# Hybrid Hyena and pooling encoder layer on one core: at the seam to the last stage, two tables asked for later, w_out piece 0 split behind the last unit, two groups reloaded as 120 and 8 partitions

## The reference

```
u    = x * (1 + scale) + shift                     # scale, shift, gate from c
proj = u @ w_in + b_in                             # 1024 -> 3072
v, x1, x2 = short_conv(proj[:, :1536])             # 3 x 512 channels
z = v
for o, g in enumerate((x1, x2)):                   # two long convolutions, 4096-point spectra
    z = g * (irfft(rfft(z) * k_freq[o])[:L] + z * bias[o])
y_h = z * silu(proj[:, 1536:2048])
y_p = pooling_mixer(proj[:, 2048:2560]) * silu(proj[:, 2560:3072])
out = gate * (concat(y_h, y_p) @ w_out + b_out)
h   = layer_norm(alpha * x + out) * ln_g + ln_b
```

## Time and profile before

| | |
|---|---|
| median of 3 runs | 1181.8 us (1180.28, 1181.8, 1186.05) |
| the profiled execution | 1175.66 us, of which the span of the trace 1173.8 us |
| TensorE busy | 1088.2 us, 93% of the span |
| VectorE busy | 850.9 us, 72% |
| ScalarE busy | 584.4 us, 50% |
| SyncE's DMA queue | 266.74 MB, 71.4% of the 16 engines' span |
| last unit's store to bseq asked for | 950.57 us |

### The profile page before, as it was taken

One profiled execution on the slowest core, in us unless ns is written; L12 is line 12 of the kernel. 1 busy time (PEld: TensorE's weight loads), 2 busy tenths in 40 slices (PEclk: granted clock), 3 DMA queues, 4 the chain that ended last, 5 costly groups with the idle time before them and its releaser, 6 DMA issues. The chain is left out here.

```text
span 1173.8 us, 14214 instructions
## 1 busy us (share of the span) xinstructions
PE 1088.2 (93%) x4928; PEld 840.9 (72%) x4928; DVE 850.9 (72%) x1081; ACT 584.4 (50%) x769; POOL 12.5 (1%) x32
## 2 busy tenths in 40 slices
PE   3799789999999999998999999898999779999996
PEld 1278668888888877766888877666788557888885
DVE  6699985555455545649999746554999957989887
ACT  4068864434545444537777635444888753222210
POOL 0001000000000000000000000000000000000000
PEclk8789999999999999999999999999999879999998
DMA  9999855677675435688999568778899999476531
GB/s 341 346 311 288 281 180 167 204 246 236 235 251 171 173 108 196 213 263 225 299 282 285 172 210 263 263 232 252 248 286 297 276 313 324 130 218 185 180 108 54
DMA packets 155132, 273.24 MB, mean 233 GB/s; under 512 B 11503, under 2 KB 49519, under 8 KB 153396
## 3 DMA queue, kind: packets, MB, share of 16 engines
q1 hardware_dynamic: 151605, 266.74, 71.4%
q0 software_dynamic: 3168, 5.51, 2.1%
q10 hardware_dynamic: 288, 0.08, 0.0%
HBM read 178.95 MB, written 98.57 MB: 236 GB/s over the span
## 5 line engine op out<-in xcount | busy, mean ns | idle before, releaser
L177 PE MATMUL u_pp<-uh_uhi,prj_whi 128*128 128x512 f32 x768 | 309.7, 403 | 14.2 <-DVE u_ulo L741 8.7
L179 PE MATMUL u_pp<-uh_uhi,prj_wlo 128*128 128x512 f32 x768 | 305.1, 397 | 0.0
L178 PE MATMUL u_pp<-u_ulo,prj_whi 128*128 128x512 f32 x768 | 304.7, 397 | 0.0
L177 PEld LDWEIGHTS u_pp<-uh_uhi,prj_whi 128*128 128x128 f32 x768 | 145.8, 190 | 57.0 <-issue 14.8
L179 PEld LDWEIGHTS u_pp<-uh_uhi,prj_wlo 128*128 128x128 f32 x768 | 145.7, 190 | 34.4
L178 PEld LDWEIGHTS u_pp<-u_ulo,prj_whi 128*128 128x128 f32 x768 | 146.1, 190 | 32.2
L1282 DVE TENSOR_TENSOR p_alo<-xin_pair,p_ahi 128x1024 fp32r<-128x1024 f32 x32 | 39.2, 1226 | 97.3 <-ACT p_ahi L1219 97.3
L1219 ACT ACTIVATE p_ahi<-xin_pair 128x1024 fp32r<-128x1024 f32 x32 | 33.9, 1060 | 124.0 <-PE p_ps L179 117.0
L593 ACT ACTIVATE fs_khi<-fs_k 128x1024 fp32r<-128x1024 f32 x32 | 34.0, 1062 | 42.2 <-DVE fs_k L570 42.2
L554 PE MATMUL fs_s<-fs_khi,flt_tab 64*128 64x512 f32 x256 | 50.6, 417 | 2.5 <-ACT prj_row L598 2.5
L177 PE MATMUL p_first<-uh_uhi,prj_whi 128*128 128x512 f32 x128 | 51.1, 399 | 1.6 <-DVE prj_wlo L2270 1.6
(11 more groups left out here) (212 smaller groups left out, 2112.0 us busy)
## 6 DMA issues: line engine op xcount, KB each, us to landing
xin_pair<-kseq SPq DMA_DIRECT2D x32, 512.0 KB, 4.3
kfreq<-xin_pair SPq DMA_DIRECT2D x32, 512.0 KB, 5.1
xseq<-p_xo SPq DMA_DIRECT2D x32, 512.0 KB, 7.7
p_k_re<-kfreq SPq DMA_DIRECT2D x64, 256.0 KB, 5.7
p_k_im<-kfreq SPq DMA_DIRECT2D x64, 256.0 KB, 4.9
bseq<-p_out SPq DMA_DIRECT2D x32, 512.0 KB, 5.1
prj_ws<-in_t_win SPq DMA_DIRECT2D x24, 512.0 KB
kseq<-prj_row SPq DMA_DIRECT2D x22, 512.0 KB, 4.1
```

Source lines behind the costliest of these rows:

```text
L177: nc.tensor.matmul(out, w[0], m[0], start=start, stop=False, skip_group_check=True)
L178: nc.tensor.matmul(out, w[0], m[1], start=False, stop=False, skip_group_check=True)
L179: return nc.tensor.matmul(out, w[1], m[0], start=False, stop=stop, skip_group_check=True)
```

## The change

Three edits in the same place.

The two tables of groups 0 and 1 were asked for at step NU - 3; they are asked for at step NU - 1, behind the store of unit 14. Piece 0 of w_out was split by ScalarE at step NU - 2 and by VectorE inside step NU - 1; both are done after the last unit's y has been split. Groups 0 and 1 were loaded whole once the store of the last unit had landed; partitions 0 to 119 are loaded once the store of unit 14 has landed, on both sides of the last store's issue, and partitions 120 to 127 after it. `high(0)` and `high(1)` wait for both parts.

```diff
--- before.py
+++ after.py
@@ -1533,8 +1533,17 @@
                 if tail and step == NU:
                     tail.load_w(sp, 4)
                     tail.load_w(sp, 5)
+                if tail and step == NU:
+                    sp.wait_ge(alo_done, NU)
+                    sp.wait_ge(stored, 16 * (NU - 1))
+                    tail.load_x_stored(sp, 0)
                 if 0 <= step - 1 < NU:
                     store(step - 1)
+                if tail and step == NU - 1:
+                    for n in range(2):
+                        tail.load_tab(sp, n)
+                if tail and step == NU:
+                    tail.load_x_stored(sp, 1)
                 q = plan.due(plan.chunk, step)
                 if q is not None and q % 4 == 2:
                     pj.load_w(sp, q // 4 + 2)
@@ -1547,8 +1556,6 @@
                 if tail and step == NU - 3:
                     tail.chunks_done(sp)
                     tail.load_quad(sp, tail.pq[0], tail.yp, tail.pq_in[0], 0)
-                    for n in range(2):
-                        tail.load_tab(sp, n)
             if tail:
                 gt.finish(sp, 4)
                 end_sync(sp)
@@ -1660,8 +1667,8 @@
                 if tail and step == NU - 2:
                     tail.chunks_done(act)
                     tail.pooled_high(act, 0, tail.pq[0])
+                if tail and step == NU - 1:
                     tail.w_high(act, 0)
-                if tail and step == NU - 1:
                     tail.w_high(act, 1)
                     tail.w_high(act, 2)
                     tail.w_high(act, 3)
@@ -1722,8 +1729,6 @@
                 if 0 <= step < NU:
                     turned(step)
                     add(step)
-                if tail and step == NU - 1:
-                    tail.w_low(dve, 0)
                 q = plan.due(plan.post, step)
                 if q is not None:
                     if q == 4 * gt.first:
@@ -1736,7 +1741,7 @@
                 if 0 <= step < NU:
                     ylow(step)
             if tail:
-                for i in range(1, 4):
+                for i in range(4):
                     tail.w_low(dve, i)
                 tail.pooled_low(dve, 1, tail.pq[0])
                 end_vector(dve)
@@ -1962,6 +1967,12 @@
 
     def load_x(self, sp, n, x):
         sp.dma_start(x, group_rows(self.bseq, n)).then_inc(self.x_in[n % 4], 16)
+
+    def load_x_stored(self, sp, n):
+        sp.dma_start(self.x[n][0:P - 8, :, :], group_rows(self.bseq, n)[0:P - 8, :, :]).then_inc(self.x_in[n], 16)
+
+    def load_x_rest(self, sp, n):
+        sp.dma_start(self.x[n][P - 8:P, :, :], group_rows(self.bseq, n)[P - 8:P, :, :]).then_inc(self.x_in[n], 16)
 
     def load_w(self, sp, i):
         after(sp, self.wlo_done[i % 4], i // 4)
@@ -2093,7 +2104,7 @@
         tail.load_w(sp, 6)
         sp.wait_ge(sp2.stored, 16 * NU)
         for n in range(2):
-            tail.load_x(sp, n, x[n])
+            tail.load_x_rest(sp, n)
         tail.load_w(sp, 7)
         load_quad(gq, g2, gq_in, gated[1], 0)
         load(2)
@@ -2195,7 +2206,7 @@
 
         def high(n):
             r = n % 2
-            act.wait_ge(x_in[n % 4], 16 * (n // 4) + 16)
+            act.wait_ge(x_in[n % 4], 16 * (n // 4) + (32 if n % 4 < 2 else 16))
             after(act, inv_done[r], n // 2)
             nc.scalar.activation(xhi[r][:, :, :], x[n % 4], ACT.Copy).then_inc(hi_done[r], 1)
```

## The result

The changed kernel is slower: 1184.54 us median over 22 runs, against 1180.85 us of the kernel before over 22 runs beside it. The ratio is 1.0033, 95% interval 1.0017 to 1.0049, that is 3.9 us (the ratios here can differ by some 0.001 from the quotient of the two medians). The forecast was 1179.3 us, within 1175.5 to 1183.5.

A forecast was written before the change was run, and what follows sets the result against it. TensorE, busy 93%, could gain only at the seam's idles, set by the DMA queue. Group 3 was taken 2.5 us earlier, between 1.3 by bytes and 3.0 to 4.0 by latencies: 1181.8 - 2.5 = 1179.3 us, range 1175.5 to 1183.5.

The forecast's parts named there:

- Part 1: Tables asked for later: k_im of unit 15 lands and its multiply starts 1.5 us earlier, bounds nothing to 2.1 us.
- Part 2: w_out piece 0 split behind the last unit: four pieces fill ScalarE's idle; last store asked for 1.45 us earlier.
- I take 5.3: Last store, behind piece 5 and 480 KB: takes 5.3 us, bounds 3.83 and 7.12, landing at 954.4.
- the slower rival: Last store stands behind the reloads, deciding from a landing at 957.4: 2.5 us late, 1184.3 us; chance 0.08.
- The small reloads: The 2 x 32 KB asked for behind the last store: land between 2.9 and 4.3 us after issue.
- The 2.1 us quoted beside that estimate: Small reloads by the skill's fixed 2.0 us plus bytes: 2.1 us each, landing at 956.6.
- I take 957.6, behind piece 6: Small reloads land at 957.6, behind w_out piece 6; ScalarE splits the two groups at about 957.9 and 959.0.
- The first is not late: Last stage's first inverse follows the pooled products ending at 960.1 without delay; the second starts at 961.6, not 964.75.
- The DMA queue decides all: Rival: the full DMA queue on both sides of the hole limits the gain to 0 to 1.3 us; chance 0.25.
- The range's other end, 1175.5: Fast end of the range: all the seam's idle goes, 5.9 us of gain; that rival's chance 0.12.
- A gain of 1.3 to 4.0 us: The forecast case for the whole kernel, with 2.5 us taken between these ends; chance 0.55.

The follow-up runs named there:

- e1: Only the two tables asked for later, against the kernel before; ratio 0.9993 (0.9972-1.0015).
- e4: Only the two groups reloaded as 120 and 8 partitions, tables and piece 0 as in the kernel before; ratio to it 1.0032 (1.0008-1.0056).
- e2: Only w_out piece 0 split later, against the kernel before; ratio 1.0002 (0.9982-1.0022).
- e3: Tables and w_out piece 0 both later, groups reloaded whole as in the kernel before; ratio to it 1.0001 (0.9978-1.0024).
- e5: Changed kernel, but ScalarE and VectorE split groups 0 and 1 ahead of w_out piece 6; ratio to the kernel before 1.0031 (1.0011-1.0050).
- e12: The same kernel as e5, run again for a second profile; ratio to the kernel before 1.0018 (1.0000-1.0037).
- e11: Changed kernel with 18 unused products ahead of the last stage's first inverse; ratio to the kernel before 1.0000 (0.9980-1.0020).
- e16: e5 with e14's unused products and ten more ahead of the last stage's first inverse; ratio to the kernel before 1.0019 (1.0003-1.0036).
- e14: e1 with 12, 8 and 16 unused products ahead of the unit loop's last three inverse transforms; ratio to the kernel before 0.9985 (0.9966-1.0004).
- e15: e14 with six more unused products between the last stage's first and second inverse; ratio to the kernel before 0.9979 (0.9957-1.0000).
- e7: The kernel before, unchanged, run again for a second profile; no ratio given, seam +55.00 us against +51.65.
- e10: Changed kernel, but group 0's 120 partitions asked for behind the last store, ahead of group 1's; ratio to the kernel before 1.0066 (1.0047-1.0086).

## Why the prediction was wrong, step by step

- **Part 1 held.** k_im's multiply at +13.52, 1.95 us earlier than before (1.5 forecast), without a wait for the transfer; e1 alone shows the same (+13.58), and no profile with the tables asked for later has that wait. Part of the size is luck: with the tables ahead of it the multiply came at +15.47, +16.12 and +16.14, but at +14.10 in e4.
- **Part 2 held.** Four pieces in a row ahead of the last copy, which then idled 0.49 us only; the last store asked for at +23.13 against +24.51, 1.38 us earlier (1.45 forecast). The times of e2 and e3 show no cost.
- **The last store's landing was mis-sized.** "I take 5.3": it was 7.1 us, the upper bound (7.12). It landed at +30.2 and not at +28.3; 1.8 us of that is its own length. The point named for the slower rival (957.4, +31.3) was not reached. The small reloads behind it kept to their bounds (2.9 to 4.3 us): in e5 they were asked for at +29.50 and ScalarE had them at +33.16. The 2.1 us quoted beside that estimate did not come. The Trainium skill (DMA: Bandwidth & Descriptors, Anatomy of one DMA) gives that fit for transfers that GpSimd asks for, and these are SyncE's.
- **The step that failed is piece 6**, "I take 957.6, behind piece 6". I gave piece 6 no landing time of its own, although it now stood behind both reloads, and had worked out the queue for the store only; the forecast needs it by 957.6 (+31.5). It took 9.7 us and not 5.1, and ScalarE started on it at +34.59 (before +30.21). ScalarE does its list in order, so the groups waited behind it. "The first is not late" was wrong by 4.40 us; against the kernel before, the first inverse starts 2.80 us later. Piece 6 is not the only thing in its place, though: with it out of the way (e5, e12) the groups are there at +33.16 and +34.22, behind the late store, and still not at the +31.5 of the forecast.
- **The clock was left out.** I had the lower clock in front of me in the earlier trace rows (0.50 from 932 to 946.5, behind idles), and did not ask what a new idle of TensorE would do to the products behind it. The sum has to hold it: the six products of an inverse start 0.43 us apart at the half clock and 0.23 at the full one. e12 against e5 puts up to 4.2 us on it; in e11, with the idle filled, the loss is gone, but in e16 it is not. The Trainium skill (TensorE: Matmul & The Clock Gate, HAM oscillation) says that waits for transfers between bursts of products throw the engine back to the low clock; the trace agrees (4.40 us idle, then 0.50 for 5.6 us). By this rule the forecast would have had a price on every idle that it was not sure of.
- **The transfers behind came as forecast and won nothing.** Group 3 was in by +46.7 at the latest (forecast +46.5, before +49.0), with the DMA engines at 393 GB/s from 970.40 to 976.00, above the 358 that the prediction quotes as a core's limit, and nobody waited for it or for the quad. "The DMA queue decides all" was wrong as a rival too: it bounded the wrong transfers. What ended last had become TensorE's own chain from the first inverse on.
- **The rival on the slow side** had the right place (reloads ahead of the last store), and the wrong transfer behind them: piece 7 instead of piece 6. It was priced at 2.5 us; measured are 3.9 us. Its own 1184.3 us lies within 0.3 us of the measured median (1184.54), which is luck, since it was reached by another path; and the range that should hold it ends at 1183.5. The range's other end, 1175.5, is not the sum either: 1181.8 - 5.9 is 1175.9.
- **The chances.** A gain of 1.3 to 4.0 us had 0.55, and the slower case 0.08. The scatter of executions (1175 to 1188 us for the kernel before over its 22 runs) I had taken for less than it is; the second profile of before has a seam 3.35 us longer than the first.

## What to carry to other kernels

A transfer that was moved ahead in the queue made those asked for right behind it late here (the store took 3.3 us more, piece 6 4.6 us more). List such requests, look up which of them stands first in an in-order engine's list, and price that one, not the one that the change is about. Price an idle of TensorE at more than its length: the products behind it may run at the half clock, and a few unused products in a wait that can't be avoided kept the clock here without a cost that the times show (e11, e14, e15). Where executions differ by as much as the change is worth, take a second profile before reading the difference of two.

## What the runs showed of the hardware

- The same wait can tip. An idle of 1.18 us left the clock at 1.00, one of 3.61 us at the same place of the same kernel was followed by the half clock, and the seam was 5.2 us longer; 2.22 us in the kernel before (e7) were followed by it too, while 1.65 us in its first profile were not. In e2 no idle ahead of the first two inverses was longer than 0.38 us, and the half clock came behind a later one, of 2.91 us, ahead of the first product.
- The landing time of a small transfer follows the crowd on the DMA engines, also from another engine's queue: 64 KB asked for by ScalarE took 2.9 us before and 5.6 us after (3.5 in e1, 4.9 in e3, which have no split).
- The last store of 512 KB took 3.8 us before, where the request ahead of it was 2.9 us old, and 7.1 us behind 480 KB of reads that were asked for 1.0 us ahead (5.9 to 7.5 us over the ten profiles with that order); with the reads behind it 4.8 us (e10), without a split 3.7 to 5.0 us.
